# The emptiest expert on 32 slots: four column tiles of 256 moved columns in the last unit

## The reference

```python
D_FF_EXPERT = 3584
N_EXPERTS = 8
TOP_K = 2

def _swiglu(x, w_gate, w_up, w_down):
    return (jax.nn.silu(x @ w_gate) * (x @ w_up)) @ w_down

def _moe(h, w_router, w_gate, w_up, w_down):
    """Top-2-of-8 expert SwiGLU; gates = softmax over the two selected router logits."""
    b, l, d = h.shape
    x = h.reshape(b * l, d)
    logits = (x @ w_router).astype(jnp.float32)
    top_v, top_i = lax.top_k(logits, TOP_K)
    gates = jax.nn.softmax(top_v, axis=-1)
    combine = jnp.sum(jax.nn.one_hot(top_i, N_EXPERTS, dtype=jnp.float32) * gates[..., None], axis=1)
    out = jnp.zeros_like(x)
    for e in range(N_EXPERTS):
        out = out + combine[:, e:e + 1].astype(x.dtype) * _swiglu(x, w_gate[e], w_up[e], w_down[e])
    return out.reshape(b, l, d)
```

## Time and profile before

| | |
|---|---|
| median of 3 runs | 1327.48 us (1326.99 to 1327.58) |
| profiled execution, its time | 1328.74 us |
| profiled execution, its span | 1326.8 us |
| busy PE, DVE, ACT | 1304.6, 795.7, 642.6 us |
| HBM read | 423.16 MB, 320 GB/s over the span |
| queue q1, which has the weights | 422.67 MB |

### The profile page before, as it was taken

How to read it: one execution, slowest core, us unless ns; L and a number is a source line. 1 busy time by engine, 2 the same in 40 slices (tenths; PEclk the granted TensorE clock), 3 DMA queues, 4 the chain that set the end, 5 groups by cost and what they waited for, 6 DMA issues and landing times.

```text
span 1326.8 us, 18843 instructions
## 1 busy us (share of the span) xinstructions
PE 1304.6 (98%) x7654; PEld 983.3 (74%) x7654; DVE 795.7 (60%) x957; ACT 642.6 (48%) x672; POOL 4.5 (0%) x12
## 2 busy tenths in 40 slices
PE   9999999999999999999999999999999999999996
PEld 8999999999999977884448885347887345888332
DVE  7564765653888679972129884118885215888122
ACT  6655644352576587761027772017774005776001
POOL 0000000000000000000000000000000000000000
PEclk9999999999999999999999999999999999999998
DMA  7335354463333499999999999999999999999995
GB/s 299 136 128 190 127 191 159 159 220 140 115 143 128 169 377 341 348 376 405 409 411 426 428 427 426 427 399 426 426 427 427 427 405 427 427 427 426 427 426 227
DMA packets 72347, 425.50 MB, mean 321 GB/s; under 512 B 6384, under 2 KB 8432, under 8 KB 27328
## 3 DMA queue, kind: packets, MB, share of 16 engines
q1 hardware_dynamic: 71680, 422.67, 78.7%
q0 software_dynamic: 432, 1.54, 0.3%
q10 hardware_dynamic: 144, 0.02, 0.0%
HBM read 423.16 MB, written 1.05 MB: 320 GB/s over the span
## 4 chain that ended last, share of the span: by engine, by line
PE 84%; DVE 9%; ACT 3%; issue 3%; DMA 1%; SPq 0%; DVEq 0%; ACTq 0%
PE ps L2388 14%; PE ps L2259 7%; PE ps L2260 7%; PE ps L2265 7%; PE ps L2419 7%; PE ps L1720 5%; PE ps L1710 4%; PE ps L1711 4%; PE ps L2284 4%; PE ps L2285 4%; PE ps L2292 4%; PE ps L1758 2%; PE ps L1775 2%; PE ps L1759 2%; DVE wl L1173 1%
## 5 line engine op out<-in xcount | busy, mean ns | idle before, releaser
L1383 DVE TENSOR_TENSOR wl<-raw,wh 128x2048 fp32r<-128x2048 f32 x96 | 218.6, 2289 | 23.9 <-ACT wh L855 23.8
L855 ACT CAST wh<-raw 128x2048 fp32r<-128x2048 f32 x96 | 183.9, 1916 | 66.8 <-PE ps L2260 40.3
L2259 PE MATMUL ps<-wh,gh 128*128 128x512 f32 x448 | 175.3, 391 | 0.7 <-DVE gl L1457 0.7
L2260 PE MATMUL ps<-wh,gl 128*128 128x512 f32 x448 | 174.4, 389 | 0.0
L918 ACT ACTIVATE sil<-ps 64x512 f32<-64x512 f32 x28 | 16.5, 589 | 299.2 <-PE ps L2390 299.2
L2388 PE MATMUL ps<-raw,few 128*64 128x512 f32 x288 | 130.2, 597 | 0.6 <-DMA raw<-in_moe_w_up 0.6
L2390 PE MATMUL ps<-raw,few 128*64 128x512 f32 x288 | 129.5, 597 | 0.0
L2265 PE MATMUL ps<-wl,gh 128*128 128x512 f32 x448 | 119.8, 389 | 0.0
L1596 DVE COPY few_act<-ps 128x256 f32<-128x256 f32 x28 | 11.9, 425 | 177.9 <-PE ps L2402 177.9
L1047 DVE TENSOR_TENSOR wl<-raw,wh 128x4096 fp32r<-128x4096 f32 (+1 forms) x18 | 73.2, 4069 | 61.7 <-ACT wh L614 39.7
L614 ACT CAST wh<-raw 128x4096 fp32r<-128x4096 f32 (+2 forms) x29 | 92.0, 3173 | 34.5 <-PE ps L1711 34.1
(11 more groups left out here) (343 smaller groups left out, 2692.0 us busy)
## 6 DMA issues: line engine op xcount, KB each, us to landing
raw<-in_moe_w_up SPq DMA_DIRECT2D x71, 1024.0 KB, 12.1
raw<-in_moe_w_gate SPq DMA_DIRECT2D x70, 1024.0 KB, 12.1
raw<-in_moe_w_down SPq DMA_DIRECT2D x51, 1024.0 KB, 13.6
unsplit<-in_moe_w_down SPq DMA_DIRECT2D x33, 1024.0 KB, 10.6
unsplit<-in_moe_w_up SPq DMA_DIRECT2D x25, 1024.0 KB, 14.2
unsplit<-in_moe_w_gate SPq DMA_DIRECT2D x22, 1024.0 KB, 17.3
raw_more<-in_moe_w_down SPq DMA_DIRECT2D x15, 1024.0 KB, 11.6
raw<-in_diff_w_qkv SPq DMA_DIRECT2D x8, 1536.0 KB, 6.6
```

What stands on the lines that cost most here:

```text
L855: act.copy(split_piece(wh, p), raw_piece(p, first)).then_inc(wh_ready, 1)
L1383: dve.tensor_tensor(split_piece(wl, p), raw_piece(p, first), raw_f(split_piece(wh, p)), ALU.subtract).then_inc(wl_ready, 1)
L2259: pe.matmul(ps[:, bank, :], gh[:, s], w, start=(k0 + k == 0), stop=False)
L2260: ins = pe.matmul(ps[:, bank, :], gl[:, s], w, start=False, stop=False)
```

## The change

The last small unit (`f == TINY_AT`, 3) holds 32 slots in place of 64. Its `up` sets the gate's 512 columns on two column tiles of 32, with 256 moved columns each, and the up part on two more; `down` sets the 1024 output columns on four tiles of 256. Each weight element is moved once as before, by twice as many matmuls of half the length. Silu, product and copies of that unit have half the columns, and it turns two blocks in place of four. Its output lies in four blocks of 32 partitions and 256 columns, so ACT copies it to `y` in four pieces, on the diagonal of a `y` that DVE has set to zero, and the scatter reads all 128 partitions. The routing sets the emptiest expert's room to 32 and keeps a list for one more unit (`MAX_UNITS` is E + 5).

```diff
-MAX_UNITS = E + 4
+MAX_UNITS = E + 5
...
+TINY = P // 4
+TINY_AT = 3
+TINY_COLS = WIDE // 2
...
@@ few_out (ACT)
-                act.copy(bm["y"][:, 0:BANK], ps[:, 2, :]).then_inc(few_y, 1)
+                if f != TINY_AT:
+                    act.copy(bm["y"][:, 0:BANK], ps[:, 2, :]).then_inc(few_y, 1)
+                    return
+                for q in range(P // TINY):
+                    s = slice(q * TINY, (q + 1) * TINY)
+                    ins = act.copy(bm["y"][s, q * TINY_COLS:(q + 1) * TINY_COLS], ps[s, 2, 0:TINY_COLS])
+                ins.then_inc(few_y, 1)
...
@@ sort_experts (DVE)
-                dve.tensor_scalar(holds[:, 1:], few, float(SMALL - P), float(P), ALU.mult, ALU.add)
+                dve.tensor_scalar(tiny, order, SORTED - 1.5, float(TINY - SMALL), ALU.is_gt, ALU.mult)
+                step(dve.tensor_scalar(holds[:, 1:], few, float(SMALL - P), float(P), ALU.mult, ALU.add))
+                dve.tensor_tensor(holds[:, 1:], holds[:, 1:], tiny, ALU.add)
...
@@ few_body (DVE)
+                    if f == TINY_AT and i == 5:
+                        dve.memset(bm["y"][:], 0.0)
...
@@ scatter_few (PE)
+                    if f == TINY_AT:
+                        to = raw_f(bm["payT"][:, (1 + f % 2) * SEQ + t * P:(1 + f % 2) * SEQ + (t + 1) * P])
+                        pe.matmul(ps[:, banks[half], :], to, bm["y"][:, half * BANK:(half + 1) * BANK], start=True,
+                                  stop=True).then_inc(sc_done, 1)
+                        continue
                     s = slice(half * SMALL, (half + 1) * SMALL)
...
@@ up (PE)
+                        if f == TINY_AT:
+                            for q in range(2):
+                                s = slice(k * WIDE + q * TINY_COLS, k * WIDE + (q + 1) * TINY_COLS)
+                                gate = pe.matmul(out_[q * TINY:(q + 1) * TINY, 0:TINY_COLS], few[:, to], few_piece(p)[:, s],
+                                                 start=first_, stop=last_, skip_group_check=True)
...
@@ down (PE)
-                        for h in range(2):
-                            s = slice(k * D + h * BANK, k * D + (h + 1) * BANK)
-                            ins = pe.matmul(ps[h * SMALL:(h + 1) * SMALL, 2, :], bm["few_act"][:, i % 2, to], few_piece(p)[:, s],
+                        for h in range(D // n):
+                            s = slice(k * D + h * n, k * D + (h + 1) * n)
+                            ins = pe.matmul(ps[h * held_:(h + 1) * held_, 2, 0:n], bm["few_act"][:, i % 2, to], few_piece(p)[:, s],
                                             start=first_, stop=last_, skip_group_check=True)
```

More of the change, by code:

```diff
@@ L402, in build, with held, few_cols @@
                 few_pieces[few_down_at(i) + half] = ("d", i, half)
+        def held(f):
+            return TINY if f == TINY_AT else SMALL
+        def few_cols(f):
+            return TINY_COLS if f == TINY_AT else WIDE
         def raw_place(s):
@@ L895, in few_tokens @@
                 act.wait_ge(few_gathered, f + 1)
-                act.copy(bm["few"][:], ps[:, 5, :]).then_inc(few_ready, 1)
+                n = KD * held(f)
+                act.copy(bm["few"][:, 0:n], ps[:, 5, 0:n]).then_inc(few_ready, 1)
             def turned_picks(f):
@@ L917, in few_body @@
                         act.wait_ge(few_prod, f * FC + i)
-                    act.activation(bm["sil"][SMALL:, :], ps[0:SMALL, i % 2, :], ACT.Silu).then_inc(few_sil, 1)
+                    n = few_cols(f)
+                    act.activation(bm["sil"][SMALL:, 0:n], ps[0:SMALL, i % 2, 0:n], ACT.Silu).then_inc(few_sil, 1)
                     if u < LAST and i in (4, 5):
@@ L1430, in pick_pair @@
             def pick_pair(u):
+                n = held(u // 2)
                 for t in range(QT):
-                    for h in range(2):
-                        ins = dve.tensor_scalar(bm["pick_few"][:, t, h * SMALL:(h + 1) * SMALL], slots[:, 0:SMALL],
+                    for h in range(P // n):
+                        ins = dve.tensor_scalar(bm["pick_few"][:, t, h * n:(h + 1) * n], slots[:, 0:n],
                                                 bm["pos_of"][:, t, u + 1:u + 2], None, ALU.is_equal)
@@ L1467, in sort_experts @@
                 middle = drawn[:, 1:]
+                tiny = bm["sort"][:, 5, 1:]
                 fuller = bm["rank"][:, 0, 0, 0:SORTED, 0:SORTED]
@@ L2199, in gather_few @@
                     pe.wait_ge(gl_ready, 2 * f + 1)
+                n = held(f)
                 for k in range(KD):
                     for t in range(QT):
-                        ins = pe.matmul(ps[:, 5, k * SMALL:(k + 1) * SMALL], bm["tok"][:, t, k * P:(k + 1) * P],
-                                        bm["pick_few"][:, t, 0:SMALL], start=(t == 0), stop=(t == QT - 1), skip_group_check=True)
+                        ins = pe.matmul(ps[:, 5, k * n:(k + 1) * n], bm["tok"][:, t, k * P:(k + 1) * P],
+                                        bm["pick_few"][:, t, 0:n], start=(t == 0), stop=(t == QT - 1), skip_group_check=True)
                 ins.then_inc(few_gathered, 1)
@@ L2399, in turn @@
                         pe.wait_ge(few_act_ready, f * FC + i)
-                    for k in range(4):
+                    for k in range(few_cols(f) // P):
                         s = slice(k * P, (k + 1) * P)
```

23 lines of the change are left out of this document (17 added, 6 removed).

## The result

| | median | lowest to highest | runs | ratio to before |
|---|---|---|---|---|
| before, same chip | 1327.53 us | 1326.99 to 1328.50 | 6 | |
| after | 1332.99 us | 1330.96 to 1334.27 | 6 | 1.0036 [1.0025, 1.0047] |

The changed kernel is slower by 0.25 to 0.47%, all of it more than the 0.2% that the measurement can tell. The time predicted was 1329.5 us, with a range up to 1332.4 us. The median of 1332.99 us lies 0.6 us above it; the ratio, set on the 1327.48 us of the prediction, gives 1332.3 us, just inside.

A forecast was written before the change was run, and what follows sets the result against it. Transfers bound the last unit, then a straight line behind the last landing. Terms -0.86 + 0.59 + 0.61 + 0.5 = +0.84 us, with +1.2 us for the clock, gave 1329.5 us from 1327.48; range 1327.5 to 1332.4 us.

The forecast's parts named there:

- what leads: Last unit: transfers lead up to the last landing, so PE time saved in its body is worth nothing.
- term 2: Last piece of down weights: four tiles side by side take its matmuls from 1.96 to 1.10 us, -0.86 us.
- PE's wait: Routing, near 505 to 545 us: PE's wait for DVE's product grows from 1.9 to 2.7 us.
- The landing: Transfer of the last piece: lands 0 to 0.8 us later than 1310.94 us.
- a sign of a wrong mechanism: Last landing: a move of more than 1.5 us would show the mechanism wrong.
- term 4: Scatter and DVE's additions: four whole-array matmuls in a row, last addition ends at 4.50 us, not 3.89, +0.61 us.
- term 6: Clock on the last piece and scatter: low for part of the tail, 0 to +4.3 us, taken as +1.2 us.
- the issue time and the norm behind it move along unchanged: Behind the last addition: the 1.99 us of issue and the norm only shift, with no added time.
- term 3: ACT's copy to `y`: four copies 0.27 us apart take 1.18 us in place of 0.59, +0.59 us.
- term 5: Routing: added DVE operations cost 0.81 us on PE, bounds 0 and 0.81, taken as +0.5 us.
- The slower rival: Tail: the clock is low through all of it, scatter matmuls at 1.71 us each, 1332.6 us; chance 0.22.

The follow-up runs named there:

- e5: The changed kernel without the count read and the branch around further wide units, on all four engines: 1330.69 us, ratio 1.0018.
- e7: The changed kernel with PE waiting for the last addition before it reads the count and branches: 1333.64 us, ratio 1.0039.
- e10: The changed kernel with two of the four copies to `y` on DVE and two on ACT: 1331.45 us, ratio 1.0027.
- e11: The changed kernel itself, run again beside the variants: 1333.68 us, ratio 1.0040.
- e12: The changed kernel with `MAX_UNITS` back at E + 4, so lists for one unit less: 1332.57 us, ratio 1.0034.
- e6: The kernel before without the count read and the branch around further wide units: 1326.01 us, ratio 0.9984.
- e1: The kernel before with only the routing's added DVE operations: 1329.33 us, ratio 1.0009.
- e3: The changed kernel with one copy of 256 columns to `y`, no memset, and a scatter of eight matmuls on four row tiles: 1328.79 us, ratio 1.0007.

## Why the prediction was partly right

**The sum of the loss.** Six profiled executions have after's last piece and scatter, without fillers (after, e5, e7, e10, e11, e12). What the clock took from the last piece and the scatter is 0, 0, 3.7, 0, 2.5 and 1.7 us, on average 1.3 us. The tail at full clock is 1.78 us longer. Their last piece starts at 1311.6 us on average; before's would start at 1309.7 us in an execution of its median time (1327.5 less 1.9 around the span less the tail of 15.9), so at some 1.9 us less. 1.3 + 1.8 + 1.9 = 5.0 us, between the 4.8 us of the ratio and the 5.5 us of the medians. The first and the last term are estimates, from few executions of several kernels, whose starts scatter by over 1 us. Forecast were +2.0 us; the 3 us that it lacks are 1.0 us of stall, 0.3 us of copies and 1.4 us of a start that came 1.9 us later and not 0.5, with 0.2 us in small pieces.

**Right: what leads.** The transfers lead (DMA share 1.01 where PE is half idle), and the body's saved PE time is worth nothing. The four tiles run side by side: term 2, -0.86 us, measured -0.85. The Trainium skill, "TensorEngine Tiling (Array Packing)", section "Theoretical Speedup", gives up to twice as much for 32 columns as for 64; the last piece agrees, 1.11 us for 1.96 with some 0.25 us of end in either. PE's wait grew to 2.6 us where 2.7 was said. The landing moved by 0.58 us between the two profiles, within the 0 to 0.8 us named, but the profile of after is its fastest execution: by the estimate above the start moves by 1.9 us at the median, which is beyond the 1.5 us that the prediction itself set as a sign of a wrong mechanism.

**Right: the scatter and the additions (term 4).** From the scatter's start to the last addition's end 4.50 us were expected, 4.49 were measured.

**Right in kind, and in size as far as six executions tell: the clock (term 6).** Taken +1.2, average 1.3 us; bounds 0 and 4.3, seen 0 to 3.7. That the guess within such wide bounds came so near is in part luck. The copies' pause does not always lose it: in after the scatter behind them is at full rate. The Trainium skill, "TensorE: Matmul & The Clock Gate", section "HAM oscillation — how this bites in real kernels", tells of a kernel in which the waits for transfers are long and each burst behind one starts at half rate. The waits for transfers named here are at most 2.6 us; behind them e7 (1.98 and 6.54 us) has the slow start and after (1.11 and 3.71 us) has not, so it is a hazard here and no rule.

**Wrong: "the issue time and the norm behind it move along unchanged".** This is the step that failed, at the end of term 4. The stall grew from 1.99 to 3.02 us, and e5 and e6 show that the branch costs 3.2 us in the new order and 2.0 us in the old. The chain of before has 1.99 us of issue in plain sight; I took it for a constant. Constant is the time from the branch line on (2.83 and 2.79 us), and before 0.85 us of it ran under the last addition. Term 4 says itself that the matmuls' results become slower than the additions; what follows from that for the branch behind them was not drawn.

**Mis-sized: the copies (term 3).** +0.59 taken, +0.90 measured. The pitch of 0.27 us came from a copy of 128 partitions with another operation behind it; these go at 0.37 us. e10 gets 0.6 us back.

**Mis-sized: the routing (term 5).** +0.5 taken, e1 has +1.25 [0, 2.4] between medians. On PE it is 0.7 us. What more there is (1.25 against 0.7 us in e1, and 1.9 us of later start in the changed kernel) was not settled: no run took apart what moves the last landing.

**The range and the chances.** The size was missed: +4.8 us by the ratio where +2.0 was forecast, at the range's very end. A slowdown beyond 0.2% had a chance of 0.36, no change that can be told 0.62. The slower rival, 1332.6 us, comes closest to the measured time, though for another reason than it gives: a clock loss near its 4.3 us (3.7) was seen in one profile of six. On average the clock takes 1.3 us, and the rest of the loss comes from the stall, the copies, the scatter and the later landing.

## What to carry to other kernels

Where transfers lead, PE's saved time is worth nothing, while idle time on PE can lower its clock for just the steps behind the last landing: cost such a change by that straight line alone, with the low clock as a price that some executions pay. A stall on the path that the profile calls issue can be the open end of a branch: find it, count its time from where the engine's sequencer is through with the branch line, ask how much of it the work before covers, and try the kernel without it (e6). Spread over more tiles, an output is best copied as it lies and scattered by tiles (e3), not moved onto a diagonal by one copy for each block.

## What the hardware showed that was not expected

- A branch over a loop that never runs takes 2.8 to 3.0 us from the branch line to DVE's next operation, in all twelve profiles that have it. On the path it costs 2.0 us in one order of the tail and 3.2 us in another. In the 10 us around it the queues named instruction move packets:

```profile
q8 instruction: 3, 0.05, 1.9%
q14 instruction: 3, 0.02, 0.7%
```

That is after, 1312.5 to 1323 us (packets, MB, share). e5 has one packet each there and e6 none, and neither has a stall. e3 moves as many as after. That a fetch of instructions is behind the 2.8 us is a guess.
- In e7 and e12 the clock was low from 1094 to 1098 us too (0.66 and 0.72), with PE busy for all of that window; in before, after and e11 it was 1.00 there. The last piece starts at 1311.28 and 1311.29 us in them and at 1311.56 and 1311.00 us in after and e11, so no cost shows.
- Four ACT copies of 32 partitions and 256 columns start 0.37 us apart, and one of 128 partitions and 256 columns takes 0.38 us: with these shapes a quarter of the partitions saves nothing.
